# The long down projection as seven products of quarters, and short-MLP weights split on chip

## The reference

```python
proj = x @ w_in + b_in
...
mix = (sigmoid(gate_lru) * y_lru + sigmoid(gate_attn) * y_attn) @ w_o + b_o
x = layer_norm(ALPHA * x + mix, ln1_g, ln1_b)
hu = depthwise_conv(x @ w_up + b_up, w_ffn_conv, b_ffn_conv, FFN_CONV_PAD)
val, gt = jnp.split(hu, 2, axis=-1)
ffn = (jax.nn.gelu(gt) * val) @ w_down + b_down
return layer_norm(ALPHA * x + ffn, ln2_g, ln2_b)
```

## Time and profile before

| | |
|---|---|
| median of 3 runs | 2669.51 us (2669.5 to 2674.13) |
| profiled execution, its span | 2675.3 us, 32667 instructions |
| PE busy | 2601.6 us, 97% |
| VectorE, ScalarE, GpSimd busy | 1629.2, 958.3, 573.8 us |
| long down projection, matmuls | 1489.2 to 1753.6 us |
| DMA read and written | 338.25 MB and 223.10 MB, 210 GB/s |

### The profile page before, as it was taken

One profiled execution on the slowest core, in us unless ns is written; L12 is line 12 of the kernel. 1 busy time (PEld: TensorE's weight loads), 2 busy tenths in 40 slices (PEclk: granted clock), 3 DMA queues, 4 the chain that ended last, 5 costly groups with the idle time before them and its releaser, 6 DMA issues.

```text
span 2675.3 us, 32667 instructions
## 1 busy us (share of the span) xinstructions
PE 2601.6 (97%) x11634; PEld 2144.6 (80%) x11634; DVE 1629.2 (61%) x2037; ACT 958.3 (36%) x1346; POOL 573.8 (21%) x306
## 2 busy tenths in 40 slices
PE   8998999999999999899999999999999999999998
PEld 6887888888778878788888888877788777888886
DVE  6899756435703649888888576467642325644445
ACT  3676713213400015444444333358732312111112
POOL 3554532232133522323232022300000000000000
PEclk9999999999999999999999999999999999999999
DMA  5665644544686843444444799976656793555544
GB/s 215 206 197 169 205 177 146 184 158 164 234 344 223 301 170 148 151 179 155 175 158 171 269 384 335 354 244 222 222 189 221 258 355 142 193 193 193 194 190 159
DMA packets 199872, 571.81 MB, mean 214 GB/s; under 512 B 16167, under 2 KB 43047, under 8 KB 197712
## 3 DMA queue, kind: packets, MB, share of 16 engines
q1 hardware_dynamic: 143712, 469.75, 48.7%
q10 hardware_dynamic: 56048, 100.59, 10.6%
HBM read 338.25 MB, written 223.10 MB: 210 GB/s over the span
## 4 chain that ended last, share of the span: by engine, by line
PE 77%; DVE 10%; DMA 7%; ACT 3%; issue 1%; ACTq 0%; SPq 0%; POOL 0%; DVEq 0%; POOLq 0%
PE ps L1182 33%; PE ps L1587 14%; PE ps L1363 8%; PE ps L1537 5%; PE ps L1457 5%; PE ps L1649 4%; DMA gate_in<-gate_dram 3%; PE ps L1226 2%; DMA raw<-w_down 2%; PE ps L1346 2%; PE ps L1396 1%; PE ps L1383 1%; DVE tau L2450 1%; DMA W<-w_split 1%; PE ps L1233 1%
## 5 line engine op out<-in xcount | busy, mean ns | idle before, releaser
L1182 PE MATMUL ps<-XH,W 128*128 128x512 f32 x2752 | 811.8, 393 | 25.6 <-POOL W L1041 10.3
L1182 PEld LDWEIGHTS ps<-XH,W 128*128 128x128 f32 x2752 | 519.4, 189 | 143.7 <-issue 11.9
L1182 PE MATMUL ps<-XL,W 128*128 128x512 f32 x1376 | 483.9, 391 | 0.0
L1182 PEld LDWEIGHTS ps<-XL,W 128*128 128x128 f32 x1376 | 260.2, 189 | 54.1
L1649 PE MATMUL ps<-Wd,Hd 128*128 128x512 f32 x1152 | 262.7, 390 | 2.1 <-DVE Hd L2919 2.0
L1649 PEld LDWEIGHTS ps<-Wd,Hd 128*128 128x128 f32 x1152 | 215.7, 188 | 48.9 <-DVE Hd L2919 3.3
L1363 PE MATMUL ps<-XH,W 128*128 128x512 f32 x672 | 216.4, 393 | 0.0
L1040 POOL TENSOR_SCALAR W<-raw 128x1024 fp32r<-128x1024 f32 (+2 forms) x72 | 88.5, 1230 | 564.1 <-PE ps L1182 295.7
L1041 POOL TENSOR_TENSOR W<-raw,W 128x1024 fp32r<-128x1024 f32 (+2 forms) x72 | 203.4, 2825 | 6.0
L1128 POOL TENSOR_TENSOR A<-raw,A 128x512 fp32r<-128x512 f32 x66 | 127.6, 1934 | 308.9 <-ACT A L2144 302.4
L1587 PE MATMUL ps<-XH,A 128*128 128x512 f32 x528 | 170.1, 390 | 0.0
(11 more groups left out here) (304 smaller groups left out, 4661.3 us busy)
## 6 DMA issues: line engine op xcount, KB each, us to landing
W<-w_split SPq DMA_DIRECT2D x130, 1024.0 KB, 6.8
w_split<-W SPq DMA_DIRECT2D x59, 1024.0 KB, 6.2
w_split<-A SPq DMA_DIRECT2D x66, 512.0 KB, 3.8
raw<-w_up SPq DMA_DIRECT2D x48, 512.0 KB, 5.7
raw<-w_down SPq DMA_DIRECT2D x48, 512.0 KB, 6.4
w_split<-Wd SPq DMA_DIRECT2D x24, 1024.0 KB, 8.4
raw<-w_qkv_mix SPq DMA_DIRECT2D x28, 512.0 KB, 4.0
h_dram<-l_h SPq DMA_DIRECT2D x24, 512.0 KB, 3.8
```

The lines of the kernel that those rows point to most:

```text
L1182: last = nc.tensor.matmul(bank(group, c), lhs(wl, k), rhs(xl, k, c), start=(k == 0 and n == 0), stop=(k == nk - 1 and n == 2))
```

## The change

The hidden features and the model columns are both halved, and so are the tokens, so that the product is one of 2x2 quarters. It is done with seven quarter products of 12 steps each (`PRODUCTS`), 84 steps. `A11`, `A12`, `A21`, `A22` are quarters of the activations, `B..` of the weights; S1 to S4 are sums of the former, T1 to T4 of the latter. A step now has a weight tile of 128x512 and 12 matmuls, in four banks of one column half. Products that share terms accumulate in the same banks, and after each of the seven VectorE adds (drains) four banks into `acc_down`.

The activations are loaded once as 1 MB chunks of four tiles (`kept`) and stay on chip; VectorE forms S1 to S4 in place, three 128x2048 operations each. GpSimd forms the weight sums, one 128x512 subtraction in each of 48 steps (`sum_w`); T1 and T2 are saved to DRAM and loaded again. GpSimd also prepares the base of tiles 4 to 7, VectorE that of tiles 0 to 3, in steps 8 to 11. Tiles 0 to 3 are normalised in steps 72 to 75. The splits lose their wait on themselves.

The long input no longer saves split down slabs or split value halves. The short MLP loads them raw, 0.5 MB for a down slab and 0.25 MB for a value half (its other half comes from `w_split` as before), and GpSimd splits them (`split_short`). PE waits for `short_split` there.

```diff
-STEPS = 2 * FT
+HALF_FT = FT // 2
+PRODUCTS = ("A11.B11", "A12.B21", "S1.T1", "S2.T2", "S4.B22", "S3.T3", "A22.T4")
+BANKS_OF = (0, 4, 4, 0, 4, 0, 0)
+FRESH = ("A11.B11", "A12.B21", "S1.T1")
+TILEWISE = ("A12.B21", "S3.T3", "A22.T4")
+W_PARTS = {"A11.B11": ("B11", None), "A12.B21": ("B21", None), "S1.T1": ("B12", "B11"), "S2.T2": ("B22", "T1"),
+           "S4.B22": ("B22", None), "S3.T3": ("T2", "B11"), "A22.T4": ("B21", "T2")}
+SAVED_SUMS = ("S1.T1", "S2.T2")
+STEPS = HALF_FT * len(PRODUCTS)
 RING = 4
+RAWS = 5
+PARTS = 4
 LAST_K = 2
+
+
+def first_step(name):
+
+    return HALF_FT * PRODUCTS.index(name)
+
+
+def product_of(s):
+
+    return PRODUCTS[s // HALF_FT]
+
+
+SUM_STEPS = [s for s in range(STEPS) if W_PARTS[product_of(s)][1]]
...
+CHUNK = 4
+S_ADDS = [(name, c) for name in ("S1", "S2", "S4", "S3") for c in range(HALF_FT // CHUNK)]
...
+        W_down = [place(f"Wd{i}", [P, 2, CH], F32R, at=form_at[n]) for i, n in enumerate(("C4", "C5", "C2", "C3"))]
+        H_down = [place(f"Hd{i}", [P, 2, CH], F32R, at=form_at[n]) for i, n in enumerate(("C6", "C7", "C0", "C1"))]
+        w_raw = [place(f"w_raw{i}", [P, CH], at=at_raw + 2048 * i) for i in range(RAWS)]
+        w_part = [place(f"w_part{i}", [P, CH], at=at_x + 48 * 1024 + 2048 * i) for i in range(PARTS)]
...
+        kept = {n: [place(f"h_{n}_{c}", [P, CHUNK, CH], at=a) for c, a in enumerate(z)] for n, z in kept_at.items()}
...
+                def load_w(s):
+
+                    name, k = product_of(s), s % HALF_FT
+                    first, second = W_PARTS[name]
+                    if s >= RAWS:
+                        sp.wait_ge(step_split, 2 * (s - RAWS) + 2)
+                        if product_of(s - RAWS) in SAVED_SUMS:
+                            sum_saved[s % RAWS].need(sp, 16 * saved_count(s - RAWS))
+                    wait_sum(first, k)
+                    sp.dma_start(w_raw[s % RAWS][:, :], w_source(first, k)).then_inc(raw_landed[s % RAWS].sem, 16)
+                    if second:
+                        n = SUM_STEPS.index(s)
+                        if n >= PARTS:
+                            w_summed.need(sp, n - PARTS + 1)
+                        wait_sum(second, k)
+                        sp.dma_start(w_part[n % PARTS][:, :], w_source(second, k)).then_inc(part_landed[n % PARTS].sem, 16)
+
+                def save_sum(s):
+
+                    if s in SUM_STEPS and product_of(s) in SAVED_SUMS:
+                        w_summed.need(sp, SUM_STEPS.index(s) + 1)
+                        sp.dma_start(t_dram["T1" if product_of(s) == "S1.T1" else "T2"][s % HALF_FT, :, :],
+                                     w_raw[s % RAWS][:, :]).then_inc(sum_saved[s % RAWS].sem, 16)
...
+                kept_at_step = {6: ("A11", 2), 9: ("A12", 0), 11: ("A12", 1), 13: ("A12", 2), 14: ("A21", 0), 15: ("A22", 0),
+                                17: ("A21", 1), 18: ("A22", 1), 20: ("A21", 2), 21: ("A22", 2), 27: ("A11", 0)}
+                for s in range(RAWS, STEPS):
+                    load_w(s)
+                    if s - 3 >= first_step("S1.T1"):
+                        save_sum(s - 3)
+                    if s == 7:
                         store_h(FT - 1)
+                    if s in kept_at_step:
+                        load_kept(*kept_at_step[s])
...
+                def fetch_mlp(free, g, n):
+
+                    slot, slab = SLOT[n], FIRST["mlp"] + 12 * g + n
+                    if n >= 2 * FG:
+                        sp.wait_ge(slab_done, free)
+                        sp.dma_start(short_raw[slot][:, :], A["w_down"][FG * g + n - 2 * FG, :, :]).then_inc(w_landed[slot], 16)
+                    elif n % 2:
+                        fetch(free, slab, slot)
+                    else:
+                        sp.wait_ge(slab_done, free)
+                        sp.dma_start(slabs[1][slot][:, :, CH:D_MODEL].bitcast(F32), w_split[slab, :, :, CH:D_MODEL]).then_inc(w_landed[slot], 16)
+                        sp.dma_start(short_raw[slot][:, 0:CH], A["w_up"][2 * FG * g + n, :, 0:CH]).then_inc(value_landed[n // 2].sem, 16)
...
+                    pool.wait_ge(rows_in[0], 48)
+                    order(pool.tensor_scalar(l_squares[:, :], l_g1[:, :], ALPHA, 1.0, ALU.mult, ALU.mult))
+                    base_made.need(pool, 1)
+                    for tt in range(4, T // P):
+                        pool.wait_ge(x_tok_in[tt % 4][0], 16 * (T // P // 4 + tt // 4 + 1))
+                        order(pool.tensor_tensor(acc_down[:, tt, :], acc_down[:, tt, :], l_squares[:, :], ALU.mult))
+                        pool.tensor_tensor(acc_down[:, tt, :], acc_down[:, tt, :], l_down[:, :], ALU.add).then_inc(base_made.sem, 1)
+
+                    def sum_w(s):
+
+                        n = SUM_STEPS.index(s)
+                        raw_landed[s % RAWS].need(pool, 16 * (s // RAWS + 1))
+                        part_landed[n % PARTS].need(pool, 16 * (n // PARTS + 1))
+                        pool.tensor_tensor(w_raw[s % RAWS][:, :], w_raw[s % RAWS][:, :], w_part[n % PARTS][:, :],
+                                           ALU.subtract).then_inc(w_summed.sem, 1)
+
...
+                    tail_after = (70, 73, 75, 77, 79, 81)
+                    for s in SUM_STEPS:
+                        sum_w(s)
+                        if s in tail_after:
+                            tail_of_short_x(tail_after.index(s))
+                    for k in range(len(tail_after), KD):
+                        tail_of_short_x(k)
...
+                def split_short(slot, width):
+
+                    head = slabs[1][slot][:, 0, 0:width]
+                    pool.sem_inc(begun, 1)
+                    order(pool.tensor_scalar(head, short_raw[slot][:, 0:width], 1.0, 1.0, ALU.mult, ALU.mult))
+                    pool.tensor_tensor(slabs[1][slot][:, 1, 0:width], short_raw[slot][:, 0:width], head.bitcast(F32),
+                                       ALU.subtract).then_inc(short_split, 1)
+
+                with order.loop(NG, 2 * FG) as g:
+                    for n in range(0, 2 * FG, 2):
+                        value_landed[n // 2].need(pool, 16 * g + 16)
+                        split_short(SLOT[n], CH)
+                    for kk in range(FG):
+                        pool.wait_ge(w_landed[DOWN_SLOT[kk]], 16 * use(1, "mlp", 2 * FG + kk, g))
+                        split_short(DOWN_SLOT[kk], D_MODEL)
...
-                        def down_tile(tt, slot, kk):
-
-                            first = down_bank(tt)
+                        def down_tile(s, t):
+
+                            name, k, slot = product_of(s), s % HALF_FT, s % RING
                             for n, (wl, xl) in enumerate(((0, 0), (0, 1), (1, 0))):
-                                for f in range(2):
-                                    last = nc.tensor.matmul(ps[:, first + f, :], H_down[slot][:, xl, (tt % 4) * P:(tt % 4 + 1) * P],
-                                                            W_down[slot][:, wl, f * CH:(f + 1) * CH],
-                                                            start=(kk == 0 and n == 0), stop=(kk == FT - 1 and n == 2))
+                                last = nc.tensor.matmul(ps[:, BANKS_OF[PRODUCTS.index(name)] + t, :],
+                                                        H_down[slot][:, xl, t * P:(t + 1) * P], W_down[slot][:, wl, :],
+                                                        start=(name in FRESH and k == 0 and n == 0),
+                                                        stop=(k == HALF_FT - 1 and n == 2), skip_group_check=True)
                             return last
...
                         def round_step(s):
 
-                            k, slot = s % 2, s % RING
-                            act.wait_ge(raw_in[k], 16 * (RAW_DOWN + s // 2 + 1))
-                            if s < 2:
+                            slot, name, k = s % RING, product_of(s), s % HALF_FT
+                            if s == 0:
                                 act.wait_ge(form_used, 7 * FAST - 7)
                                 act.wait_ge(form_saved[0][0], FORM_BASE + 24 * FAST)
                             elif s < RING:
-                                act.wait_ge(form_used, 7 * FAST if s == 3 else 7 * FAST - 1)
+                                act.wait_ge(form_used, 7 * FAST - 7 if s == 1 else 7 * FAST - 1)
                             else:
                                 act.wait_ge(step_used, s - 3)
-                                saves = min(s, FT) // RING if s % 2 == 0 else max(0, s - FT) // RING
-                                act.wait_ge(w_saved[slot], 16 * (TOTAL[0][slot] + saves))
-                            A1(W_down[slot][:, 0, :], raw[k][:, 0:D_MODEL], ACT.Copy).then_inc(down_rounded, 1)
-                            act.wait_ge(h_landed[slot][0], H_BASE + 16 * (s // RING + 1))
-                            A1(H_down[slot][:, 0, :], H_down[slot][:, 1, :].bitcast(F32), ACT.Copy).then_inc(down_rounded, 1)
+                            if s in SUM_STEPS:
```

(57 more changed lines are left out.)

409 lines of the change are left out of this document (208 added, 201 removed).

## The result

The changed kernel takes 2692.4 us (median of 4 runs, 2692.2 to 2694.6) against 2669.5 of the kernel before (2668.5 to 2674.1). The ratio is 1.0088, 95% interval 1.0074 to 1.0102: 23 us slower, where 1.4 were forecast and 2684 was the end of the range. The profiled execution of the changed kernel took 2692.2 us, as its median; its span from first to last instruction is 2689.6. The span of the kernel before, 2675.3, already lies 5.8 above that kernel's median, so its trace is of a slow execution. The two spans therefore differ by 14.3 us only.

A forecast was written before the change was run, and what follows sets the result against it. TensorE, busy 97%, was taken as the bound, with VectorE feeding the changed stage. Stage 264.7 us against 264.8 before (-0.1), plus 1.5 behind it, gave +1.4 us on 2669.5: 2671 us, range 2651 to 2684.

The forecast's parts named there:

- 230 us floor: Long down stage: TensorE's least time for 84 steps of 2.74 us, 32.8 us less through 144 fewer matmuls.
- the four places of loss: Long down stage: TensorE idle near steps 2, 8 to 11, 24 to 43 and 72 to 75.
- dearer-splits rival: Long down stage: a split costs VectorE 0.73 us, not 0.60; 11.7 us more, total 2683; chance 0.17.
- The feed keeps up: Rival, long down stage: GpSimd's sums land on drains and idle moments; total 2650, or 2656 at half price; chance 0.35.
- short-MLP rival: Short MLP: fetches with their waits exceed the margin by 1 to 2 us in five groups, 5 to 10 us; chance 0.09.
- Points 1 and 2: Stage start to step 8: step 2's split done at 8.9 us, wanted at 5.5; broadcast rows landed at 25.
- Points 3 and 4: Steps 8 to 24: split 11 done at 46.4 us, split 24 at 86.4; 20.7 us lost up to here.
- Points 5 and 6: Steps 24 to 43: VectorE 59.5 us against TensorE's 54.7, 4.8 lost; nothing lost from there through step 71.
- Point 7: Steps 72 to 75: layer-norm tiles stand ahead of drains that TensorE awaits; step 75 starts 9.2 us late.
- The short MLP, charged 0: Short MLP: GpSimd's split of the third slab stays hidden, with a margin of 0.8 to 2.3 us; no loss.
- Clock gaps, charged 0: Long down stage: gaps could lower TensorE's clock, but the three long ones fall where VectorE is the bound; 0 us.
- +1.5 behind the stage: After the long down stage: the last tiles are written later, delaying ScalarE's start on the short sequence by 1.5 us.

The follow-up runs named there:

- a1_short_unsplit: Changed kernel, but the short MLP's slabs are loaded in two halves from other slabs and GpSimd splits nothing there (other weights computed): 2682.2 us.
- b3_short_dve: Changed kernel, but in the short MLP ScalarE rounds and VectorE subtracts the down slabs, fetched in a6_short_order's order: 2684.8 us.
- b1_stage_dve: Changed kernel, with weight sums (one step ahead) and base of tiles 4 to 7 on VectorE, base of tiles 0 to 3 at steps 12 to 15: 2672.8 us.
- a4_norm_late: Changed kernel, with the layer norm of tiles 0 to 3 at steps 76 to 79 in place of 72 to 75, stores four steps later: 2695.5 us.
- a6_short_order: Changed kernel, with only the order of the short MLP's slab fetches and GpSimd splits altered, slab 8 fetched ahead of 6 and 7: 2693.5 us.
- a7_sum_dummy: Changed kernel with weight sums over 8 of 512 columns, each followed by a 512-wide GpSimd subtraction that nobody reads: 2690.5 us.

## Why the prediction was wrong

**Right in kind.** The removed matmuls, the 230 us floor (84 x 2.72 = 228.5 measured), the prices and the four places of loss. A sum cost VectorE 1.01 us of busy time and a 1024-wide instruction 1.94, where 1.09 and 2.18 were taken; in steps 24 to 43 the sums cost 16 us, where 20 x 1.09 less 3.5 hidden, 18.3, were charged. The dearer-splits rival fell: unblocked splits still show 0.68, and in the changed kernel's trace they start 0.60 us apart:

```profile
1541.65 0.68 DVE L3058 TENSOR_TENSOR Wd<-w_raw,Wd 128x512 fp32r<-128x512 f32 x1
1542.25 0.68 DVE L3061 TENSOR_TENSOR Hd<-h_A,Hd 128x512 fp32r<-128x512 f32 x1
1542.85 0.68 DVE L3058 TENSOR_TENSOR Wd<-w_raw,Wd 128x512 fp32r<-128x512 f32 x1
```

"The feed keeps up" fell too. The short-MLP rival named the right place with the wrong mechanism (late fetches in five groups; what was lost lies in the first and the last).

**Points 1 and 2, the start.** Step 2 starts at 8.3 us (forecast 8.9). The rows land at 28.0, not 25.

**Points 3 and 4, steps 8 to 24.** 27.8 us are lost up to step 24, not 20.7: I charged 7 too little. Split 11 is done at 53.2, not 46.4. 3.0 of this are the rows. The rest is that I put one of GpSimd's base tiles into steps 8 to 11, and two lay there: splits 8, 9 and 10 are done 7.9 us apart, 2.5 + 1.2 of VectorE's own and 4.2 of GpSimd's. From split 11 to 24 VectorE then took 37.2 us, not 40.0, and idled once TensorE was behind it.

**Points 5 and 6.** Steps 24 to 43 lose 6.1 (forecast 4.8) and the stretch behind 0.4. VectorE's 60.6 us from split 24 to 44 meet the 59.5 worked out.

**Point 7, steps 72 to 75.** 13.3 lost, not 9.2. Split 71 was done 5.5 us before step 72 was due, not 8.3, and the first drain came 15.8 after it, not 12.2. Most of it is GpSimd: without its sums this part loses 4.8. I had given the two norm tiles and two splits 3.3 us of its share. The stage is thus a matter of sizes: 7.1, 1.3, 0.4 and 4.1 us more in these parts, 0.9 at its end, less 1.5 for the floor, are the 12.3 by which it ran over.

**The short MLP, charged 0, cost 12.5.** This is the step that failed by kind, and it is half of the 24.8 us by which the two places ran over. I asked only whether GpSimd's halves come in time for TensorE, "with VectorE out of the way". They nearly do: the wait for them is 2.3 us. I did not ask what 96 GpSimd instructions do to VectorE there (67.4 us more of busy time, 1792.7 against 1725.3 in a1_short_unsplit), though the same prediction had priced exactly that for the stage. A down slab's two instructions last 1.36 + 2.61 us, and VectorE has 26 us of its own work in 50. It absorbs them in the middle groups, and not in the first, where it has the residual base besides, nor in the last, where the down is only two tiles wide and uses up each slab in 2.7 us. That GpSimd is the cause is shown (a1_short_unsplit, b3_short_dve); why just these two groups can't absorb it is my reading of the timelines.

**Clock gaps, charged 0.** No run takes this apart from the waits; by my reading it was nearly right in the stage. TensorE was granted 0.67 and 0.74 in the windows from 1520 and 1720, a mixture of its two levels, 1.2 and 2.4 GHz, after waits of 7.3 and 10.1 us. Its 1008 matmuls were busy 242.7 us where 228.5 would do. But the splits set the pace: 8 to 10 are done as their steps start. Step 10 lasts 4.5 us with split 11 done after 3.7, step 72 4.7 us with split 73 long done; the next late splits, 18 and 74, for which TensorE waits again, take both up. In the first group of the short MLP it was not 0: about 1.8 us. The slower matmuls also hide part of the loss from the page: the waits add up to 34.3 us, while the steps lost 48.6. That the 34.3 are so close to the 34.7 forecast is luck.

**The sum.** Stage +12.3 and short MLP +12.5 make 24.8, and the two ends take 0.8 off. Between the stage and the short MLP, where both kernels do the same work, the trace of the kernel before lost 9.7 us more than the changed one's, which leaves the 14.3 between the spans. Part of that can be seen: its granted clock was 0.91 from 1834 to 1894 us, against 1.00 in the same stretch of the changed kernel (1845.6 to 1905.6):

```profile
1834.00:1894.00 60.00, 54.12 (x219) 43.56 (x218) 46.54 (x68) 53.87 (x71) 0.00 (x0) 0.91 0.58 191
```

As that execution was slow against its kernel's median, by 5.8 us in its span alone, I take the 9.7 for its own and not for a gain of the change; by the medians the kernels lie 22.9 us apart, 8.6 more than the spans. This is argued, as there is one trace of the kernel before. My +1.5 behind the stage can't be read at this size.

**What stays open.** How much of the 3 us ahead of the first group is GpSimd's first two up halves and how much their place in the load queue was not tried apart; a1_short_unsplit removes both. What the lower clock alone costs, and how the 20 us of b1_stage_dve divide among its three edits, was not tried either.

## What to carry to other kernels

Before work goes to GpSimd, ask two questions: when is its result ready, and what does VectorE do meanwhile. Where VectorE set the pace, on tensors in SBUF, the work was cheaper on VectorE itself (0.71 us for a sum against 1.01); but placed two steps ahead, often before their operands had landed, the same sums gave nothing (2691.5 us). And a gain in TensorE's floor (32.8 us here) has to be set against the engine that feeds it at the new, shorter step; moving its work about mostly moved the wait (a4_norm_late, a6_short_order).

## What the runs showed of the hardware

A GpSimd instruction that VectorE waits for in no way slows it too: each dummy of a7_sum_dummy cost it 0.75 us of busy time (1780.2 against 1744.3 us for 48), a real sum 1.01, and in steps 24 to 43 both cost 16 us. GpSimd is slowed in turn. In that kernel's trace a 1.74 us subtraction takes 3.33 while VectorE adds 2048 columns without a break:

```profile
1628.99 3.33 POOL L1251 TENSOR_TENSOR l_down<-l_g 128x512 f32<-128x512 f32 x1
```

```profile
1628.89 2.28 DVE L3090 TENSOR_TENSOR h_A<-h_A,h_A 128x2048 f32<-128x2048 f32 x1
1631.10 0.68 DVE L3113 TENSOR_TENSOR acc_down<-ps,acc_down 128x512 f32<-128x512 f32 x1
1631.81 1.06 DVE L3061 TENSOR_TENSOR Wd<-w_raw,Wd 128x512 fp32r<-128x512 f32 x1
```

The drain between them, with an operand in PSUM, keeps its 0.68 us; the split behind it is the one that stretches. The Trainium skill, SBUF — State Buffer, section "SBUF: two separate sides", describes a lock on the ports that the two engines share, taken for an instruction at a time; these rows agree with it, in both directions.
